# Fused mixer, expert lookup and delta-rule block: the 128x128 block inverses taken in two pairs of token blocks with the scan beside them, and the attention's division moved behind its value product

## Chip, cores and metric

The kernel runs on one core of a Trainium2 chip. The metric is the device time of one launch in microseconds. All data are f32; the big linear layers split every operand in two parts of fewer bits (`_hi` and `_lo`) and make three products of them, the smaller products named below are plain f32 products, which the profile counts as two matmul records each (a transpose is one record).

## What is computed

A first block (gated convolutions, a linear recurrence, a product-key expert lookup over 16384 experts) and then a second block, which alone is touched here. Its input is 512 tokens of width 1024; half of its width is causal attention with ALiBi slopes, the other half a gated delta rule:

```
moba_out = moba_attention(a_q, a_k, a_v) * silu(a_z)        # 8 heads of 64; 512 tokens: plain causal softmax
gdn_out  = rms_norm(gated_delta_rule(...), w) * silu(d_z)   # 4 heads of 128
mixed    = concat([moba_out, gdn_out]) @ w_out
return x + rms_norm(mixed, norm_post_w)

# gated delta rule, per chunk:
a     = strict_lower((k*beta) k^T * decay);  t_inv = (I + a)^-1
u     = t_inv @ (v*beta);   w = t_inv @ (k*beta*exp(gc))
v_new = u - w @ S
o     = (q*exp(gc)) @ S + intra @ v_new
S     = S*exp(g_last) + (k*exp(g_last - gc))^T @ v_new      # chunk after chunk
```

The attention's softmax is exp(logit - max), a sum over keys, and a division by the sum.

## The kernel before

Every engine runs its own instruction list; semaphores tie them together. For the second block all five lists are written by walking over one table, `STEPS2` (built by `second_block_steps`), so the table sets the order on every engine at once; an engine that has no part in a step passes over it. The stage of interest starts when the 32 input projections (`unit` 0 to 31) are over and ends with the first output projection (`unit` 32).

The 512 tokens are four blocks of 128 (`tb` 0 to 3); the delta rule's four heads of one block are handled together. Its steps:

- `M(level, tb)` and `X(level, tb)`: the inverse of I + a by doubling, 7 levels (0 to 6). `M` is eight 64x64 products (at level 6 four); ScalarE copies the result from PSUM to `M1[:, tb % 2]`; `X` is sixteen 64x64 products (level 6: four) with that copy; VectorE subtracts the result from the inverse. GpSimd writes the masked operand of the next level to `AO[:, tb % 2]` (`mask`). So a block's level is a circle: `M` on TensorE, copy on ScalarE, `X` on TensorE, subtraction on VectorE. At each level all four blocks pass, in the order M0 M1 X0 M2 X1 M3 X2 X3.
- `tokens(tb)`: transposes of k and v; VectorE makes `KB` and `VB` (4 + 4 `tensor_scalar`, one for each head, L2402), and ScalarE the decayed k (4 activations, L1817).
- `solve` (products w and u, copied by ScalarE), `read` (w @ S, VectorE subtracts: L2558), `scan` (o, and the product `su` that VectorE adds to the state: L2570, 4 instructions), `gsquare` (ScalarE's squares with sums, 4 instructions for each block, L1844), `groot` (ScalarE's square root L1850, VectorE's reciprocal and 12 or 4 scalings L2583), `gturn` (16 transposes, L1440, and four VectorE products L2588).
- `values(q)`: transposes of the attention's v.

The attention is cut into 32 pieces n (m = n // 8 a pair of heads, query block qb = n // 2 % 4, e = n % 2 the head), spread over 36 slots, one for each call of `attend()`, placed between the steps above. Slot i holds, in this order: `pv` of pieces i-5 and i-4 (odd i: the value product of both heads, L1471), `turn` of piece i-3 (transposes of the probabilities to PSUM bank 7, L1459, copied by ScalarE, L1865), `both_logits` of i and i+1 (even i, L1452), `logits` i (VectorE adds the slopes and takes the extreme, L2605; ScalarE takes exp with the sum, L1854), `probs` i-1 (VectorE's reciprocal L2610; ScalarE multiplies the row with it, L1859). After every eighth piece, at slots 11, 19, 27 and 35, the result of a head pair is gated and split: VectorE `tmp` (L2618), ScalarE `act_hi` (L1535), VectorE `act_lo` (L1914, in `rest`). This is called the head-pair switch below. Since VectorE works in order, the `logits` of that slot come after `act_lo`, and the next `both_logits` waits for them (`nm_ready`).

Small results share four PSUM banks in turn (`JOBS`, `bank`): job n waits with `wait_free` until job n-4 has been read (`emptied`).

## Time and profile before

| | |
|---|---|
| median of 3 runs | 1854.47 us (1851.41 to 1855.57) |
| the profiled execution's own time | 1854.16 us |
| its span in the trace | 1852.4 us |
| TensorE busy | 1792.7 us (97%) |
| VectorE, ScalarE, GpSimd busy | 1500.4, 721.3, 1048.3 us |
| stage from the first attention product to unit 32 | 1676.15 to 1789.69 us |

The profile's busy times count each instruction from start to end; TensorE's ends are modelled, and its instructions overlap a little, so for the cost of a group in a row the distance to the next group's start is the better measure (a group given with 1.10 us is followed 1.03 us later). `[0.58 <-DVE small L2605]` behind a row means that the engine stood idle 0.58 us before it and that this instruction released it. The clock column is the granted TensorE clock; 1.00 is 2.4 GHz, 0.50 is 1.2 GHz.

### The profile page before, as it was taken

To read this page: it belongs to the slowest core of one execution; us is meant where nothing else is said; L and a number is where in the kernel's file an instruction comes from. 1 tells how busy PE (TensorE), PEld (TensorE's weight loads), DVE (VectorE), ACT (ScalarE), POOL (GpSimd) and SP (SyncE) were. 2 spreads that over 40 slices of the span, in tenths; PEclk is the share of its full clock that TensorE was granted. 3 is DMA by queue.
4 is the path that set the end of the run, shared out by engine and by line. 5 is a ranking of instruction groups with operands and counts; after the bars stand their busy time and mean duration, and the time that the engine had idled before them with its cause. 6 is when DMAs were issued, how large, how long until landed. Compare 5 with 4: busy or idle time off the path is not lost.

```text
span 1852.4 us, 28952 instructions
## 1 busy us (share of the span) xinstructions
PE 1792.7 (97%) x10379; PEld 1566.0 (85%) x10379; DVE 1500.4 (81%) x2496; ACT 721.3 (39%) x1166; POOL 1048.3 (57%) x653
## 2 busy tenths in 40 slices
PE   7999999999999999999999999999999999999986
PEld 5788879999999999999888888888888686787765
DVE  5786899879998888888489999999999796655544
ACT  3454233333333444344333333333333434325652
POOL 1442355788888555555567777676775463336013
PEclk9999999999999999999999999999999999999998
DMA  9551524899999699899899999999997232210011
GB/s 373 202 172 57 185 77 137 280 318 318 327 319 312 233 305 320 296 309 318 326 339 360 362 356 363 349 363 357 368 353 273 69 92 79 69 57 2 2 57 57
DMA packets 159933, 440.48 MB, mean 238 GB/s; under 512 B 13664, under 2 KB 62944, under 8 KB 156768
## 3 DMA queue, kind: packets, MB, share of 16 engines
q1 hardware_dynamic: 64416, 254.71, 39.7%
q0 software_dynamic: 36864, 134.23, 19.3%
q10 hardware_dynamic: 58560, 50.34, 8.3%
q8 instruction: 54, 0.88, 0.2%
q14 instruction: 39, 0.32, 0.0%
HBM read 386.80 MB, written 52.43 MB: 237 GB/s over the span
## 4 chain that ended last, share of the span: by engine, by line
PE 88%; DVE 6%; DMA 2%; ACT 2%; issue 1%; SPq 0%; ACTq 0%; DVEq 0%
PE PS L974 15%; PE PS L983 15%; PE PS L975 15%; PE PS L1272 9%; PE PS L1273 9%; PE PS L1281 9%; PE PS L1239 4%; PE PS L1317 2%; PE PS L1001 1%; DMA arena<-in_w_ada 1%; PE PS L1308 1%; DVE arena L1946 1%; PE PS L1459 1%; PE PS L1452 1%; DMA gates_d<-arena 1%
## 5 line engine op out<-in xcount | busy, mean ns | idle before, releaser
L862 POOL TENSOR_TENSOR w_lo<-raw,w_hi 128x1024 fp32r<-128x1024 f32 x299 | 720.0, 2409 | 693.2 <-ACT w_hi L1502 692.2
L1502 ACT ACTIVATE w_hi<-raw 128x1024 fp32r<-128x1024 f32 x332 | 352.1, 1060 | 923.3 <-PE PS L983 570.7
L974 PE MATMUL PS<-act_hi,w_hi 128*128 128x384 f32 (+1 forms) x1584 | 576.4, 364 | 2.2 <-DVE act_lo L1914 0.7
L975 PE MATMUL PS<-act_lo,w_hi 128*128 128x384 f32 (+1 forms) x1584 | 562.8, 355 | 0.0
L983 PE MATMUL PS<-act_hi,w_lo 128*128 128x384 f32 (+1 forms) x1584 | 337.2, 354 | 0.0
L974 PEld LDWEIGHTS PS<-act_hi,w_hi 128*128 128x128 f32 x1584 | 299.0, 189 | 34.9 <-DVE act_lo L2379 4.9
L975 PEld LDWEIGHTS PS<-act_lo,w_hi 128*128 128x128 f32 x1584 | 299.1, 189 | 23.3 <-issue 2.6
L1272 PE MATMUL PS<-w_hi,act_hi 128*128 128x512 f32 x768 | 300.4, 391 | 3.4 <-ACT arena L1658 3.4
L983 PEld LDWEIGHTS PS<-act_hi,w_lo 128*128 128x128 f32 x1584 | 284.5, 188 | 22.6 <-issue 0.5
L1273 PE MATMUL PS<-w_hi,act_lo 128*128 128x512 f32 x768 | 300.2, 391 | 0.0
L2326 DVE TENSOR_TENSOR act_lo<-arena,act_hi 128x384 fp32r<-128x384 f32 x128 | 249.1, 1946 | 29.6 <-ACT act_hi L1716 29.6
L1281 PE MATMUL PS<-w_lo,act_hi 128*128 128x512 f32 x768 | 195.2, 389 | 0.0
L2181 DVE CUSTOM_DVE_ANT_0 arena<-arena,PS 128x1024 f32<-128x1024 f32 x128 | 153.8, 1213 | 25.5 <-DMA arena<-in_expert_u_rows,arena 25.2
L1272 PEld LDWEIGHTS PS<-w_hi,act_hi 128*128 128x128 f32 x768 | 145.0, 189 | 33.8 <-ACT arena L1658 3.7
L1273 PEld LDWEIGHTS PS<-w_hi,act_lo 128*128 128x128 f32 x768 | 145.0, 189 | 30.1
L1281 PEld LDWEIGHTS PS<-w_lo,act_hi 128*128 128x128 f32 x768 | 144.6, 188 | 30.1
L2298 DVE SCALAR_TENSOR_TENSOR PS<-arena,PS 128x1024 f32<-128x1024 f32 x127 | 162.4, 1279 | 0.5
L910 POOL DMA_INDIRECT arena<-in_expert_v,arena x128 | 134.9, 1054 | 24.8 <-issue 19.4
L2285 DVE TENSOR_TENSOR arena<-PS,arena 128x1024 f32<-128x1024 f32 x96 | 117.2, 1221 | 36.3 <-PE PS L1239 32.9
L910 POOL DMA_INDIRECT arena<-in_expert_u_rows,arena x128 | 122.4, 956 | 32.1 <-issue 12.0
L1239 PE MATMUL PS<-arena 128*128 128x128 f32 x768 | 93.5, 275 | 0.6 <-ACT arena L1694 0.4
L1239 PEld LDWEIGHTS PS<-arena 128*128 128x128 f32 x768 | 92.2, 191 | 1.1 <-ACT arena L1694 0.8
(358 smaller groups left out, 1913.2 us busy)
## 6 DMA issues: line engine op xcount, KB each, us to landing
raw<-in_expert_u SPq DMA_DIRECT2D x128, 512.0 KB, 5.4
raw<-in_expert_v SPq DMA_DIRECT2D x128, 512.0 KB, 5.9
raw<-in_w_in SPq DMA_DIRECT2D x52, 512.0 KB, 3.7
arena<-in_w_ada SPq DMA_DIRECT2D x24, 1024.0 KB, 9.6
gel_d<-arena ACTq DMA_DIRECT2D x64, 384.0 KB
gates_d<-arena ACTq DMA_DIRECT2D x12, 2048.0 KB, 15.4
arena<-gates_d SPq DMA_DIRECT2D x32, 768.0 KB, 7.0
arena<-gel_d SPq DMA_DIRECT2D x32, 768.0 KB, 8.8
```

The source lines that it names most:

```text
L862: pool.tensor_tensor(w_lo[:, k % SPLIT, :], raw[:, k % RAW, :], w_hi[:, k % SPLIT, :].bitcast(F32), ALU.subtract).then_inc(lo_split, 1)
L910: pool.indirect_dma_start(out=rows[buffer(s)], out_offset=None, in_=table, in_offset=bass.IndirectOffsetOnAxis(ap=row_i[:, s % SLOTS:s % S ...
L974: pe.matmul(own, w, act_hi[:, c, 0:n_tok], start=(i == 0), stop=False)
L975: pe.matmul(own, w, act_lo[:, c, 0:n_tok], start=False, stop=False)
L983: mm = pe.matmul(own, w_lo[:, k % SPLIT, c * P:(c + 1) * P], act_hi[:, c, 0:n_tok], start=False, stop=(i == KC - 1))
L1239: mm = pe.matmul(PS[:, 2 + g % 3, t * P:(t + 1) * P], hot[:, n, 0, :], hot[:, n, 1, :], start=True, stop=True)
L1272: pe.matmul(to, coef(act_hi, k)[:, q, :], w, start=start, stop=False, skip_group_check=True)
L1273: pe.matmul(to, coef(act_lo, k)[:, q, :], w, start=False, stop=False, skip_group_check=True)
L1281: mm = pe.matmul(PS[:, 2 * q + half, :], coef(act_hi, k)[:, q, :], w_lo[:, k % SPLIT, 512 * half:512 * half + 512], start=False, stop=stop ...
L1502: act.activation(w_hi[:, k % SPLIT, :], raw[:, k % RAW, :], ACT.Copy).then_inc(hi_split, 1)
L2298: v.scalar_tensor_tensor(out=own_ps, in0=rows[buffer(s)], scalar=dots[:, k:k + 1], in1=own_ps, op0=ALU.mult, op1=ALU.add).then_inc(rows_us ...
L2326: v.tensor_tensor(coef(act_lo, b % 4), craw[:, b % 2, :].rearrange("p (q t) -> p q t", q=GT), coef(act_hi, b % 4).bitcast(F32), ALU.subtra ...
```

## The change

1. Inverse. After level 0, which is as before, blocks 0 and 1 go through levels 1 to 6 alone (`invert_two(0, ...)`), then blocks 2 and 3. `tokens` 0 and 1 stand at the end of the first pair; `solve` 0 and 1, `read` 1, `scan` 0 and 1 and their `gsquare`, and `tokens` 2 and 3 stand inside the second pair's levels. Behind the inverse only blocks 2 and 3 are left of the scan.
2. Division. `probs` issues nothing any more. `turn` takes the undivided exp. One `precip` for each head pair takes 8 reciprocals at once; `prow` spreads them over 64 output rows for each head with 8 products against the identity (out 64x128), VectorE multiplies this into the gate `az`, and the switch multiplies the value product by that.
3. Tokens. `KB`, `VB` and the decayed k are three VectorE instructions of 128x512 with the scalars broadcast; ScalarE's four are gone. The k bank is free after the third.
4. Squares. `gsquare` of blocks 0 to 2 is one VectorE product and one reduction; block 3 stays on ScalarE.
5. The semaphore counts follow the table (`x_done`, `COPIED`, `MASKED`, `same_buffer_before`).

```
+        if i >= 10 and i % 8 == 2:
+            steps.append(("precip", i // 8 - 1))
         if i >= 4 and i % 2:
+            if i % 8 == 3 and i > 8:
+                steps.append(("prow", i // 8 - 1))
             steps.append(("pv", i - 4))
...
+    def invert_two(tb, between):
+
+        for level in range(1, LEVELS):
+            product(level, tb)
+            if level > 1:
+                steps.append(("X", level - 1, tb + 1))
+            steps.extend(between.get((level, 0), ()))
+            attend()
+            steps.append(("X", level, tb))
+            product(level, tb + 1)
+            steps.extend(between.get((level, 1), ()))
+            attend()
+        steps.append(("X", LEVELS - 1, tb + 1))
+
+    invert_two(0, {(5, 0): [("tokens", 0)], (6, 0): [("tokens", 1)]})
+    invert_two(2, {(1, 0): [("solve", 0)], (2, 0): [("read", 0), ("scan", 0), ("gsquare", 0)], (3, 0): [("solve", 1)],
+                   (3, 1): [("read", 1)], (4, 1): [("scan", 1), ("gsquare", 1)], (5, 0): [("tokens", 2)],
+                   (6, 0): [("tokens", 3)]})
+    for kind, n, count in (("solve", 2, 1), ("read", 2, 1), ("solve", 3, 0), ("scan", 2, 2), ("read", 3, 2), ("scan", 3, 2)):
         steps.append((kind, n))
         if kind == "scan":
             steps.append(("gsquare", n))
             if n == 3:
                 steps.append(("groot", 1))
-        if kind in ("tokens", "read", "scan"):
+        for _ in range(count):
             attend()
         if (kind, n) == ("read", 3):
             steps.append(("groot", 0))
...
-                    "kt": (tok_act, n + 1), "vt": (tok_dve, n + 1),
+                    "kt": (kd_ready, n + 1), "vt": (tok_dve, n + 1),
...
                 if kind == "turn":
-                    pe.wait_ge(p_ready, n + 1)
+                    pe.wait_ge(e_ready, n + 1)
...
+                if kind == "prow":
+                    pe.wait_ge(r_ready, n + 1)
+                    wait_free(pe, "pr", n)
+                    for q in range(TB):
+                        for e in range(2):
+                            k = 8 * n + 2 * q + e
+                            mm = pe.matmul(PS[64 * e:64 * e + 64, bank("pr", n), q * P:(q + 1) * P],
+                                           prec[:, k:k + 1].to_broadcast([P, 64]), ident[:, :], start=True, stop=True)
+                    full(mm, "pr", n)
...
-                if kind == "probs":
-                    w = (n // 2 % 4 + 1) * P
-                    act.wait_ge(r_ready, n + 1)
-                    act.activation(L[:, n % 3, 0:w], L[:, n % 3, 0:w], ACT.Copy, scale=prec[:, n:n + 1]).then_inc(p_ready, 1)
...
-                    per_head(KB[:, tb % 2, :], ("kt", tb), bge, 4 * tb)
-                    per_head(VB[:, tb % 2, :], ("vt", tb), beta, 4 * tb, last=tok_dve)
+                    own, kt = slice(4 * tb, 4 * tb + 4), h4(PS[:, bank("kt", tb), :])
+                    wait_full(dve, "kt", tb)
+                    v.tensor_tensor(h4(KB[:, tb % 2, :]), kt, by_head(bge[:, own]), ALU.mult)
+                    wait_full(dve, "vt", tb)
+                    v.tensor_tensor(h4(VB[:, tb % 2, :]), h4(PS[:, bank("vt", tb), :]), by_head(beta[:, own]),
+                                    ALU.mult).then_inc(tok_dve, 1)
+                    v.tensor_tensor(cv[:, 4:8, t], kt, by_head(egcum[:, 32 + 4 * tb:36 + 4 * tb]), ALU.mult).then_inc(kd_ready, 1)
...
+                if kind == "gsquare" and n < TB - 1:
+                    dve.wait_ge(o_ready, n + 1)
+                    chain.link(v.tensor_tensor(gscratch[:, :, :], otok[:, :, t], otok[:, :, t], ALU.mult))
+                    v.tensor_reduce(gsum[:, 4 * n:4 * n + 4], gscratch[:, :, :], AX_X, ALU.add).then_inc(gsq_ready, 1)
...
+                if kind == "prow":
+                    if n == 0:
+                        dve.wait_ge(z_done, 8)
+                    wait_full(dve, "pr", n)
+                    v.scalar_tensor_tensor(out=az[:, n, :], in0=PS[:, bank("pr", n), :], scalar=0.5, in1=az[:, n, :],
+                                           op0=ALU.mult, op1=ALU.mult).then_inc(gate_scaled, 1)
+                if kind == "precip":
+                    dve.wait_ge(e_ready, 8 * n + 8)
+                    v.reciprocal(prec[:, 8 * n:8 * n + 8], psum_[:, 8 * n:8 * n + 8]).then_inc(r_ready, 1)
```

**Order, TensorE at the third head-pair switch (slot 27).** In the kernel before, L1471 is `pv` of pieces 22 and 23, L1459 `turn` 24, L1426 and L1427 the eight products of `scan` 1, and L1308 its `su`; `turn` 25 and the next logits follow behind it.

```order
L1471 MATMUL PS<-arena,raw 64x128 [waits pt_ready]
L1471 MATMUL PS<-arena,raw 64x128 x7
L1459 MATMUL PS<-ident,arena 128x128 [waits pt_ready,p_ready]
L1426 MATMUL PS<-arena 128x128 [waits tok_dve,vn_ready]
L1427 MATMUL PS<-arena 128x128
```

In the changed kernel L1507 is `prow` 2, L1520 `pv`, L1499 `turn` 24 and 25, L1492 `both_logits` 28; the row ahead of L1507 is `su` of block 2.

```order
L1348 MATMUL PS<-arena 128x128 [waits vn_ready,kd_ready]
L1348 MATMUL PS<-arena 128x128 x3
L1507 MATMUL PS<-ident,small 64x128 [waits wu_ready,r_ready]
L1507 MATMUL PS<-ident,small 64x128 x7
L1520 MATMUL PS<-arena,raw 64x128 [waits pt_ready]
L1520 MATMUL PS<-arena,raw 64x128 x7
L1499 MATMUL PS<-ident,arena 128x128 [waits pt_ready,e_ready] x2
L1492 MATMUL PS<-arena 128x384 [waits nm_ready]
```

The scan's products stood behind the switch and stand ahead of it now; two turns and the next logits follow each other directly.

**Order, VectorE at the same place.** In the changed kernel L2609 adds `su` of block 2 to the state, L2615 and L2616 are the squares, L2655 is `prow`, L2666 `tmp`, L1945 `act_lo`, L2648 the logits of piece 27 (before, L2618, L1914 and L2605 stood with nothing of the scan ahead but L2558).

```order
L2609 SCALAR_TENSOR_TENSOR arena<-arena,small,PS 128x128 [waits bank_full2]
L2609 SCALAR_TENSOR_TENSOR arena<-arena,small,PS 128x128 x3
L2615 TENSOR_TENSOR arena<-arena 128x512 [waits o_ready]
L2616 TENSOR_REDUCE small<-arena 128x4 [waits dve_chain]
L2655 SCALAR_TENSOR_TENSOR arena<-PS,arena 128x512 [waits bank_full3]
L2666 TENSOR_TENSOR arena<-PS,arena 128x512 [waits pv_done,gate_scaled,alo_ready]
L1945 SCALAR_TENSOR_TENSOR act_lo<-arena,act_hi 128x512 [waits tmp_ready,ahi_ready]
L2648 ISA arena,small<-arena,PS 128x256 [waits pt_full,s_full]
```

The state, the squares and the spread sums now come ahead of the switch's `tmp` in this list.

**Order, ScalarE at the end of the stage.** Before: L1854 is the exp of piece 31, L1859 the last divisions, L1850 the square roots, L1844 the squares of block 3, L1865 the copies of `turn` 29 to 31.

```order
L1854 ACTIVATE arena,small<-arena,small 128x512 [waits nm_ready]
L1859 ACTIVATE arena<-arena,small 128x512 [waits r_ready]
L1850 ACT_TABLE_LOAD
L1850 ACTIVATE small<-small 128x12 [waits gsq_ready]
L1844 ACTIVATE arena,small<-PS 128x128 [waits bank_full2,gsq_ready]
L1844 ACTIVATE arena,small<-PS 128x128 [waits gsq_ready] x3
L1850 ACTIVATE small<-small 128x4 [waits gsq_ready]
L1865 ACTIVATE arena<-PS 128x384 [waits pv_done,pt_full]
```

Now: L1889 is exp (first row piece 30, last row piece 31), L1885 the square roots, L1879 the squares, L1896 the copies of `turn` 28 and 29.

```order
L1889 ACTIVATE arena,small<-arena,small 128x512 [waits nm_ready]
L1885 ACT_TABLE_LOAD
L1885 ACTIVATE small<-small 128x12 [waits gsq_ready]
L1879 ACTIVATE arena,small<-PS 128x128 [waits bank_full5,gsq_ready]
L1879 ACTIVATE arena,small<-PS 128x128 x3
L1885 ACTIVATE small<-small 128x4 [waits gsq_ready]
L1896 ACTIVATE arena<-PS 128x384 [waits pv_done,pt_full]
L1889 ACT_TABLE_LOAD
L1889 ACTIVATE arena,small<-arena,small 128x512 [waits nm_ready]
L1896 ACTIVATE arena<-PS 128x384 [waits pv_done,pt_full]
```

The square roots moved from behind the last exp to ahead of it; one more function table is loaded for that exp, and another for the square root at the kernel's very end (L1875 before, L1906 now).

## Rows read from the trace of the kernel before

**Rows 1.** Busy time by stretch: each engine's busy us, clock, DMA share, GB/s.

```profile
core 0 of [0], span 1852.4 us
...
1671.50:1676.15 4.65, 2.28 (x20) 1.69 (x17) 4.56 (x9) 2.72 (x5) 1.90 (x2) 1.00 0.00 0
1676.15:1742.44 66.29, 62.26 (x1220) 49.23 (x1219) 37.51 (x136) 42.01 (x121) 26.12 (x20) 0.97 0.01 3
1742.44:1770.43 27.99, 26.41 (x232) 23.09 (x231) 12.83 (x47) 21.54 (x68) 0.00 (x0) 1.00 0.01 2
1770.43:1789.69 19.26, 13.98 (x99) 10.47 (x97) 10.14 (x34) 9.93 (x31) 0.00 (x0) 0.82 0.00 0
1789.69:1852.40 62.71, 48.10 (x224) 39.08 (x222) 26.30 (x32) 18.34 (x28) 20.53 (x11) 0.91 0.25 84
```

**Rows 2.** The same view for two stretches at the lower clock.

```profile
1731.50:1735.30 3.80, 3.80 (x52) 2.91 (x48) 2.29 (x8) 2.30 (x8) 0.00 (x0) 0.55 0.00 0
...
1779.30:1786.10 6.80, 5.81 (x29) 4.56 (x30) 5.53 (x18) 1.13 (x3) 0.00 (x0) 0.51 0.00 0
```

**Rows 3.** Timeline of TensorE: start, us, instruction, idle time before it.

```profile
1700.79 1.61 PE L1317 MATMUL PS<-arena 64*64 64x64 f32 x48
1702.33 1.10 PE L1471 MATMUL PS<-arena,raw 128*64 128x128 f32 x16
...
1705.14 0.30 PE L1459 MATMUL PS<-ident,arena 128*128 128x128 f32 x1 [0.37 <-ACT arena L1865]
1706.02 0.92 PE L1452 MATMUL PS<-arena 64*128 64x384 f32 x4 [0.58 <-DVE small L2605]
...
1763.08 0.92 PE L1452 MATMUL PS<-arena 64*128 64x384 f32 x4
...
1767.17 0.44 PE L1459 MATMUL PS<-ident,arena 128*128 128x128 f32 x2
...
1770.75 1.13 PE L1452 MATMUL PS<-arena 64*128 64x512 f32 x4
1771.86 1.13 PE L1308 MATMUL PS<-arena 128*128 128x128 f32 x8
...
1778.71 0.30 PE L1440 MATMUL PS<-ident,arena 128*128 128x128 f32 x1 [2.54 <-DVE arena L2583]
```

**Rows 4.** Timeline of VectorE.

```profile
1703.47 0.69 DVE L2618 SCALAR_TENSOR_TENSOR arena<-PS,arena 128x512 f32<-128x512 f32 x1 [0.67 <-PE PS L1471]
1704.93 0.69 DVE L1914 SCALAR_TENSOR_TENSOR act_lo<-arena,act_hi 128x512 fp32r<-128x512 f32 x1 [0.77 <-ACT act_hi L1535]
1705.54 0.41 DVE L2605 CUSTOM_DVE_ANT_0 arena<-arena,PS 128x256 f32<-128x256 f32 x1
...
1725.81 2.15 DVE L2402 TENSOR_SCALAR raw<-PS,small 128x128 f32<-128x128 f32 x8
...
1763.08 1.12 DVE L2570 SCALAR_TENSOR_TENSOR arena<-arena,small,PS 128x128 f32<-128x128 f32 x4 [0.36 <-PE PS L1308]
...
1778.27 2.44 DVE L2583 TENSOR_SCALAR arena<-arena,small 128x128 f32<-128x128 f32 x12
...
1780.84 1.13 DVE L2583 TENSOR_SCALAR arena<-PS,small 128x128 f32<-128x128 f32 x4
```

**Rows 5.** Groups of VectorE over the span: the reduction of 512 columns.

```profile
L2269 DVE TENSOR_REDUCE arena<-arena 128x32 f32<-128x512 f32 x1 | 0.7, 686 | 3.1 <-ACT arena L1684 3.1
```

**Rows 6.** Timeline of ScalarE.

```profile
1704.20 0.63 ACT L1535 ACTIVATE act_hi<-arena 128x512 fp32r<-128x512 f32 x1 [0.92 <-DVE arena L2618]
...
1776.38 1.28 ACT L1850 ACT_TABLE_LOAD   x1
1777.67 0.30 ACT L1850 ACTIVATE small<-small 128x12 f32<-128x12 f32 x1
...
1836.85 0.26 ACT L1875 ACTIVATE arena<-PS,small 128x4 f32<-128x4 f32 x1 [1.14 <-PE PS L1014]
```

**Rows 7.** Groups of ScalarE from 1676.15 to 1789.69 us: the divisions.

```profile
L1859 ACT ACTIVATE arena<-arena,small 128x128 f32<-128x128 f32 (+3 forms) x32 | 17.7, 552 | 2.4 <-DVE small L2610 2.4
```

More of the change, by code:

```diff
@@ L114, in second_block_steps @@
     fill = 30
-    for level in range(LEVELS):
-        for what, tb in (("M", 0), ("M", 1), ("X", 0), ("M", 2), ("X", 1), ("M", 3), ("X", 2), ("X", 3)):
-            if (what, level) == ("X", 0):
-                steps.append((what, level, tb))
-            if what == "X":
-                if fill < 32:
-                    steps.append(("unit", fill))
-                elif fill == 33:
-                    steps += [("values", q) for q in range(TB)]
-                    attend()
-                elif fill > 33 and not (level == 6 and tb % 2):
-                    attend()
-                fill += 1
-            if (what, level) != ("X", 0):
-                steps.append((what, level, tb))
-            if (what, level, tb) in (("X", 5, 1), ("X", 6, 1)):
-                steps.append(("tokens", level - 5))
-            if what == "M" and 4 * level + tb + 2 < 4 * (LEVELS - 1):
-                steps.append(("mask", level + (tb + 2) // 4, (tb + 2) % 4))
@@ L136, in second_block_steps, with product @@
-    for kind, n in (("solve", 0), ("tokens", 2), ("solve", 1), ("read", 0), ("scan", 0), ("tokens", 3), ("solve", 2),
-                    ("read", 1), ("scan", 1), ("solve", 3), ("read", 2), ("scan", 2), ("read", 3), ("scan", 3)):
+    masks = iter([(0, 2), (0, 3)] + [(level, pair + tb) for pair in (0, 2) for level in range(1, LEVELS - 1) for tb in (0, 1)])
+    def product(level, tb):
+        steps.append(("M", level, tb))
+        if level < LEVELS - 1:
+            steps.extend(("mask", *at) for at in itertools.islice(masks, 1))
@@ new lines, in second_block_steps @@
+    for what, tb in (("M", 0), ("M", 1), ("X", 0), ("M", 2), ("X", 1), ("M", 3), ("X", 2), ("X", 3)):
+        if what == "M":
+            product(0, tb)
+        else:
+            steps.append(("X", 0, tb))
+            if tb < 2:
+                steps.append(("unit", 30 + tb))
+    steps += [("values", q) for q in range(TB)]
+    attend()
[9 more added lines that the diff above has]
+            steps.extend(between.get((level, 1), ()))
+            attend()
+        steps.append(("X", LEVELS - 1, tb + 1))
@@ L208, with x_done, same_buffer_before @@
 NAMES = list(JOBS)
+X_STEPS = [st[1:] for st in STEPS2 if st[0] == "X"]
+M_STEPS = [st[1:] for st in STEPS2 if st[0] == "M"]
+COPIED = [at for at in M_STEPS if at[0]]
+MASKED = [st[1:] for st in STEPS2 if st[0] == "mask"]
+def x_done(level, tb):
+    return TB + X_STEPS.index((level, tb)) + 1
+def same_buffer_before(order, level, tb):
+    own = [at for at in order if at[1] % 2 == tb % 2]
+    return own[own.index((level, tb)) - 1]
 class Chain:
@@ L949, in _ @@
                     if n or tb >= 2:
-                        before = (n, tb - 2) if tb >= 2 else (n - 1, tb + 2)
+                        before = same_buffer_before(MASKED, n, tb)
                         if before[0]:
@@ L953, in _ @@
                         else:
-                            pool.wait_ge(d_ready, TB + before[1] + 1)
+                            pool.wait_ge(d_ready, x_done(*before))
                     pool.tensor_tensor(h4(AO[:, tb % 2, :]), h4(AT[:, tb, :]),
@@ L1809, in _ @@
                     wait_full(act, "m", n, tb)
-                    act.wait_ge(d_ready, 4 * n + tb + 3)
+                    act.wait_ge(d_ready, x_done(*same_buffer_before(X_STEPS, n, tb)))
                     own = slice(0, P) if n < LEVELS - 1 else HI
                     act.activation(M1[own, tb % 2, 0:256], PS[own, bank("m", n, tb), 0:256], ACT.Copy).then_inc(m1_ready, 1)
-                if kind == "tokens":
-                    wait_full(act, "kt", tb)
-                    act.wait_ge(tok_dve, tb + 1)
-                    for h in range(GH):
-                        ins = act.activation(cv[:, 4 + h, t], PS[:, bank("kt", tb), h * P:(h + 1) * P], ACT.Copy,
-                                             scale=egcum[:, 32 + 4 * tb + h:33 + 4 * tb + h])
-                    ins.then_inc(tok_act, 1)
                 if kind == "solve":
@@ L1848, in _ @@
                     own = slice(0, 12) if n == 0 else slice(12, 16)
-                    act.wait_ge(gsq_ready, own.stop)
+                    act.wait_ge(gsq_ready, TB - 1 + 4 * n)
                     act.activation(grms[:, own], gsum[:, own], ACT.Sqrt, bias=eps, scale=1.0 / P).then_inc(g_root, 1)
```

61 lines of the change are left out of this document (28 added, 33 removed).

## Prediction

> **What bounds the kernel now.** I read the stretches first, then TensorE's timeline in them, then the lists of the engines it waits for. Outside the stage from 1676.15 to 1789.69 us the two programs issue the same steps, but for one table load at the end. The stage takes 113.54 us, and TensorE is busy in most of it: it is idle for 4.03, 1.58 and 5.28 us in its three stretches, 10.9 us together [rows 1]. In two places it also ran at the lower of its two levels, 1.2 GHz: a clock of 0.55 over 3.80 us costs 1.7 us, and 0.51 over 6.80 us, part of which was waiting anyway, about 2.5 us [rows 2]. That leaves 113.5 - 10.9 - 4.2 = 98.4 us of products at full clock, so the stage is bound by TensorE's own work, with 15.1 us to be had from waits and clock. The waits are short ones at the head-pair switch (0.37 and 0.58 us), where TensorE needs a copy and logits that stand behind `tmp`, `act_hi` and `act_lo`, and one of 2.54 us ahead of `gturn`, for VectorE's scalings behind the square root [rows 3]. The lower clock follows both kinds: a run of short waits before 1731.5 and the long one before 1779.3.
>
> **What the change adds.** `prow` is the only new work on the bound engine: 4 times 8 products of 128x128 onto 64 output rows. The nearest row is `pv` with 16 records, the same output, 1702.33 to its end 1.03 us on [rows 3]. A floor is half of it, a ceiling twice it (2 to 8 us); I take 4 x 1.03 = **4.1 us**, since size and record count are the same.
>
> **What it takes away, and who notices.** 32 divisions leave ScalarE (17.7 us [rows 7]) and the turns wait for one step less. But ScalarE is busy for 42.01 of 66.29 us in the first stretch and TensorE for 62.26 [rows 1]: the relief lies beside products and gives nothing by itself. The tokens stay as they are for VectorE (8 scalings 2.15 us; now three of 128x512, each 0.6 to the next start like 1704.93 to 1705.54 [rows 4], so 1.8 us and one more bank release at their end). GpSimd's masks are the same 22, in another order.
>
> **Two blocks in flight.** A block's circle is M 0.5 (a third of the 1.54 us that 48 records take), a copy, X 1.0, subtractions: about 3.0 us with hand-overs, an estimate. TensorE's period for one level of two blocks is 2 x 1.54 [rows 3] plus two attention slots of about 1 us: 5.1. So the circle has 2.1 us of slack, and the levels should stay filled. Exposed places, in program order:
>
> A. Level 1: X0 came behind M0 and M1 and comes behind M0 alone; the copy it needs is late by what M1 covered: +0.5.
>
> B. First switch, slots 11 and 12, right behind `tokens` 1. Counted from the end of X(5,1), VectorE has subtractions 1.2, tokens to 3.1, the gate times `prow` to 3.7, then `tmp` to the logits 2.07 us (1703.47 to 1705.54 [rows 4]) and 0.48 to the next `both_logits` (1705.54 [rows 4] to 1706.02 [rows 3]): 6.3. TensorE has in it about 4.7 us of work (transposes 1.0, `prow` and `pv` 2.06, two small turns 0.5, two steps of level 6 at an estimated 0.6). Wait 1.6.
>
> C. Last levels of the second pair. Between `su` 1 and M(5,3) VectorE must do state 1.1, squares 1.4, logits 0.3, subtractions 0.8, tokens 1.9: 5.5 us, because the k bank is now released by the third token instruction; TensorE has 4.9 there. Wait 0.6. At `tokens` 3 the same list delays logits 23, its exp and the copy of M(6,3): 0.9. Together 1.5.
>
> D. Behind `su` of block 2. The order shows that `prow`, `pv`, two turns and the next logits follow without cover, where `scan` 1 stood between before; and VectorE has state, squares and `prow` ahead of `tmp`. From the end of that `su`: state 1.1 [rows 4], squares 0.69 + 0.69 ([rows 5] for the reduction), less overlap 1.35, gate 0.6, switch 2.07, 0.48: **5.6 us**, against 2.6 us of TensorE's work. Wait 3.0. Then everything hangs in a line: logits 28 0.85, the read of block 3 0.95, value product and turn 0.4 each, 0.5 for a copy, turn 0.4, logits 30 1.06 [rows 3]: 10.1. Logits and exp of piece 30 1.6: 11.7. Table load and root up to the first scaling 1.89 (1776.38 [rows 6] to 1778.27 [rows 4]), the scalings 3.6 to the end of the last four: 17.2. Only now come logits 31 and its exp (1.55) and the copy of turn 29 (0.5), which stands behind that exp on ScalarE: 19.3. `pv` 29 0.8, turn 30 0.6, copy 0.7, turn 31 0.6, `prow` 3 over the copy 1.03, `pv` 31 1.03: **24.1 us** to unit 32. Before, the last `su` ended at 1770.43 and unit 32 began 19.26 us later [rows 1].
>
> **The table load.** Exp, root, exp makes two more loads than exp, root: one for exp 31, one for the root at the kernel's end. A load is 1.28 us, and the root begins 0.01 us after it [rows 6]. The first falls in the time in which ScalarE waits for logits 31. The second must fit in the 1.14 us that the last root waits [rows 6]: +0.15. The Trainium skill (ScalarE: Activation LUTs, What ACT_TABLE_LOAD costs) puts a drain of about 1.38 us beside each load, 2.66 us for a switch; this trace shows no such gap at this load. By the page the end would cost 1.5 instead of 0.15.
>
> **The sum.** Work outside the last stretch is 98.4 less that stretch's 11.5 (19.26 - 5.28 - 2.5), 86.9. Of it 3.2 us (`pv` 23 and 25, three turns, logits 28) move into D; two `prow` come in, 2.06; waits A, B, C 3.6. That is 89.4, with D 113.5 at full clock, where before it was 113.54. So without the clock the stage breaks even: what the waits of before give back, `prow` takes. For the clock I take two falls of 1.85, 3.7 us, since D has waits of 3.0, 2.2 (turn 29 behind the squares and root) and 1.9 us (`pv` 29), and one of 2.54 brought the clock down. Bounds: none, and 6 us. Total +3.7 + 0.15 = +3.8 on the profiled execution's own 1854.16 (the median is 1854.47, 0.3 above): **1858.0 us**, +0.2%.
>
> **Rivals.**
>
> Break-even: the same waits, but clock falls that lie in time that waits anyway, as in `gturn`, and slots that fill B. Then -2.5 to +1. For it: the 0.95 us of waits at the first switch cost no clock, since the whole first stretch ran at 0.97 [rows 1], which the 3.80 us of [rows 2] nearly account for.
>
> Faster: the switch and the square root are hidden. If of my waits only A, C and one of 2.3 us remain and the clock stays up, the stage is 98.4 + 4.1 + 4.3 = 106.8: -6.7, from -4 to -8. For it: ScalarE loses 17.7 us and half the scan is inside the levels. Against: the scan's cover is what it takes away from the tail, and squares of block 2 stand before the switch. It decides if VectorE's list at D is not late by more than 0.6 us.
>
> Starved levels: with two blocks instead of four, ScalarE's exp and turn copies stand between a product and its copy. Each 0.1 us over the 2.1 of slack in 24 half levels is 2.4 us; 0.25 gives +6 more, +9.8. Against: the in-order lists leave the copy ahead of the exp of the same slot.
>
> The drain: ScalarE would wait at each load, D longer by up to 1.4 and the end by 1.4: +5.2 to +6.6. The page named above gives this rule; the row's 0.01 us speaks against it.
>
> No effect of the regrouping, only `prow`: +4, inside the forecast's case.
>
> **How the numbers follow.** Forecast +1 to +7: 0.48. Break-even 0.24. Faster 0.14. Starved 0.09. Drain 0.05. About 0.2%, 3.7 us, is what a measurement can tell from no change. Faster by more: 0.14. Slower by more: half of the forecast's case 0.24, starved 0.09, drain 0.05: 0.38. The same: 0.48. The range runs from 1852.0, which leaves out the faster case, to 1863.0, which leaves out most of the starved one; the forecast's own is 1855 to 1861.
>
> **What the trace of the changed kernel would show.** `prow` at about 1.0 us each; hardly any idle TensorE between 1680 and 1695; a wait of 1 to 2 us at the first switch; after `su` of block 2 some 3 us of waiting released by ScalarE's copy and VectorE's logits; turn 29 and `pv` 29 waiting for ScalarE about 2 us each; a granted clock of 0.5 in one or two stretches behind these; a table load ahead of exp 31 that nobody waits for, and one ahead of the last root. The forecast is wrong if VectorE reaches the third switch's `tmp` on time, if the clock stays up, or if TensorE is idle in the levels themselves.

## The result and the profile after

The changed kernel takes 1859.78 us (median of 10 runs, 1856.68 to 1863.12), the kernel before in the same comparison 1854.63 (10 runs, 1850.73 to 1857.12): a ratio of 1.003, 95% interval 1.0021 to 1.0039. It is 5.2 us slower; the forecast was 3.8 us slower, inside its range, on the side that had 0.38 of the chance. The profiled execution took 1859.47 us, its span 1857.7.

First the stretches of the changed kernel (columns as in [rows 1]). The first three rows are the stage, cut at the end of the inverse and at the end of `su` of block 2; the fourth is what comes behind it, the fifth the whole stage. The last three are the stretches at the lower clock, cut by hand and a little short at their ends.

```profile
1676.15:1759.06 82.91, 78.23 (x1366) 63.69 (x1365) 45.89 (x128) 37.38 (x104) 26.54 (x20) 0.96 0.01 2
1759.06:1769.05 9.99, 9.99 (x90) 9.11 (x88) 1.94 (x7) 5.39 (x13) 0.00 (x0) 1.00 0.01 2
1769.05:1794.85 25.80, 19.12 (x158) 14.39 (x156) 15.16 (x44) 11.40 (x31) 0.00 (x0) 0.87 0.00 1
1794.85:1857.70 62.85, 48.12 (x224) 39.08 (x222) 26.30 (x32) 19.61 (x29) 20.54 (x11) 0.92 0.24 84
1676.15:1794.85 118.70, 107.34 (x1609) 87.20 (x1608) 62.99 (x179) 54.18 (x147) 26.54 (x20) 0.94 0.01 2
1676.90:1683.50 6.60, 5.97 (x93) 5.01 (x89) 1.68 (x8) 2.42 (x9) 3.17 (x4) 0.50 0.01 2
1775.90:1779.10 3.20, 3.17 (x14) 2.21 (x14) 1.21 (x3) 0.71 (x2) 0.00 (x0) 0.50 0.00 0
1786.20:1789.30 3.10, 3.10 (x14) 2.83 (x15) 3.06 (x13) 1.52 (x2) 0.00 (x0) 0.50 0.02 5
```

The stage starts where it did and lasts 118.70 instead of 113.54 us: 5.16 of the 5.3 us by which the span grew. TensorE is idle for 4.68 us in the levels and 6.68 in the last stretch, 11.4 against 10.9 [rows 1]. The middle stretch, where the block scan stands beside the last attention pieces, has no idle time at all. The granted clock is 0.94 of full over the stage, with three stretches at half clock; before it was 0.95, with the two of [rows 2].

TensorE's timeline, from level 1, from the first switch (slots 11 and 12), from the end of the levels, and from the third switch to unit 32 (a row's number before the engine is its us, the bracket the idle time ahead of it and who ended it):

```profile
1678.14 2.08 PE L1357 MATMUL PS<-arena 64*64 64x64 f32 x34 [0.63 <-ACT arena L1861]
...
1707.23 1.09 PE L1507 MATMUL PS<-ident,small 128*64 128x128 f32 x16 [0.53 <-DVE arena L2579]
...
1711.31 0.30 PE L1499 MATMUL PS<-ident,arena 128*128 128x128 f32 x1 [0.96 <-ACT arena L1896]
1712.06 0.92 PE L1492 MATMUL PS<-arena 64*128 64x384 f32 x4 [0.44 <-DVE small L2648]
...
1747.64 0.63 PE L1375 MATMUL PS<-ident,arena 128*128 128x128 f32 x4 [1.02 <-ACT arena L1861]
...
1758.45 0.68 PE L1357 MATMUL PS<-arena 64*64 64x64 f32 x8 [0.76 <-ACT arena L1861]
...
1769.13 1.09 PE L1507 MATMUL PS<-ident,small 128*64 128x128 f32 x16
1770.05 1.04 PE L1520 MATMUL PS<-arena,raw 128*64 128x128 f32 x16
1771.03 0.33 PE L1499 MATMUL PS<-ident,arena 128*128 128x128 f32 x1
1774.03 0.30 PE L1499 MATMUL PS<-ident,arena 128*128 128x128 f32 x1 [2.68 <-ACT arena L1896]
1774.92 0.92 PE L1492 MATMUL PS<-arena 64*128 64x384 f32 x4 [0.58 <-DVE small L2648]
...
1779.63 0.41 PE L1499 MATMUL PS<-ident,arena 128*128 128x128 f32 x2 [0.56 <-ACT arena L1896]
...
1786.18 0.87 PE L1499 MATMUL PS<-ident,arena 128*128 128x128 f32 x3 [2.03 <-ACT arena L1896]
1786.84 3.27 PE L1480 MATMUL PS<-ident,arena 128*128 128x128 f32 x16
1790.16 0.88 PE L1520 MATMUL PS<-arena,raw 128*64 128x128 f32 x12
```

Each of the four groups of `prow` is followed 0.90 to 0.93 us later: 3.7 us. The largest wait is the one behind the third switch, 2.68 + 0.58 us; VectorE and ScalarE say why:

```profile
1769.24 1.12 DVE L2609 SCALAR_TENSOR_TENSOR arena<-arena,small,PS 128x128 f32<-128x128 f32 x4 [4.24 <-PE PS L1348]
1770.28 0.68 DVE L2615 TENSOR_TENSOR arena<-arena 128x512 f32<-128x512 f32 x1
1770.99 0.69 DVE L2616 TENSOR_REDUCE small<-arena 128x4 f32<-128x512 f32 x1
1771.60 0.68 DVE L2655 SCALAR_TENSOR_TENSOR arena<-PS,arena 128x512 f32<-128x512 f32 x1
1772.37 0.69 DVE L2666 TENSOR_TENSOR arena<-PS,arena 128x512 f32<-128x512 f32 x1
1773.83 0.69 DVE L1945 SCALAR_TENSOR_TENSOR act_lo<-arena,act_hi 128x512 fp32r<-128x512 f32 x1 [0.77 <-ACT act_hi L1584]
1774.44 0.41 DVE L2648 CUSTOM_DVE_ANT_0 arena<-arena,PS 128x256 f32<-128x256 f32 x1
```

```profile
1746.52 0.62 ACT L1889 ACTIVATE arena<-arena,small 128x384 f32<-128x384 f32 x1 [2.56 <-DVE small L2648]
...
1747.13 0.36 ACT L1861 ACTIVATE arena<-PS 128x256 f32<-128x256 f32 x1
...
1773.09 0.63 ACT L1584 ACTIVATE act_hi<-arena 128x512 fp32r<-128x512 f32 x1 [4.15 <-DVE arena L2666]
1773.63 0.26 ACT L1896 ACTIVATE arena<-PS 128x128 f32<-128x128 f32 x1
...
1782.70 1.28 ACT L1885 ACT_TABLE_LOAD   x1
1783.99 0.30 ACT L1885 ACTIVATE small<-small 128x12 f32<-128x12 f32 x1
...
1786.05 1.28 ACT L1889 ACT_TABLE_LOAD   x1
1788.91 0.72 ACT L1889 ACTIVATE arena<-arena,small 128x512 f32<-128x512 f32 x1 [1.58 <-DVE small L2648]
...
1841.00 1.28 ACT L1906 ACT_TABLE_LOAD   x1
1842.30 0.26 ACT L1906 ACTIVATE arena<-PS,small 128x4 f32<-128x4 f32 x1
```

State, squares, spread sums and `tmp` run one behind the other without a gap. ScalarE stands still for 4.15 us ahead of `act_hi`, and the copy of turn 24 (L1896 at 1773.63), for which TensorE's turn 25 waits, is queued behind it. So TensorE waits for a copy of 0.26 us, but what is late is VectorE's list.

### The profile page after: what moved, and what is told of

Same layout as the page of the kernel before. It is cut to its first block and busy times, and to the rows that moved or that the text cites. A ratio compares the mean times of both kernels' runs of the same rounds, so it can differ in the third digit from the quotient of the medians.

```text
span 1857.7 us, 28970 instructions
## 1 busy us (share of the span) xinstructions
PE 1798.1 (97%) x10443; PEld 1570.1 (85%) x10443; DVE 1505.1 (81%) x2458; ACT 703.4 (38%) x1096; POOL 1050.2 (57%) x653
```

## The experiments

Twelve kernels, each timed beside the kernel before; an interval is the 95% interval of the ratio to it. The theory at the start was that of the prediction: TensorE pays for `prow`, the relief of ScalarE gives nothing by itself, and the regrouping costs waits in the last stretch and the clock that falls behind them.

**The division put back in the changed kernel.** `precip` and `prow` are taken out, `probs` issues again.

```
-        if i >= 10 and i % 8 == 2:
-            steps.append(("precip", i // 8 - 1))
-            if i % 8 == 3 and i > 8:
-                steps.append(("prow", i // 8 - 1))
-                    pe.wait_ge(e_ready, n + 1)
+                    pe.wait_ge(p_ready, n + 1)
+                if kind == "probs":
+                    act.wait_ge(r_ready, n + 1)
+                    act.activation(L[:, n % 3, 0:w], L[:, n % 3, 0:w], ACT.Copy, scale=prec[:, n:n + 1]).then_inc(p_ready, 1)
```

> The changed kernel with the division alone put back: ScalarE multiplies each row of probabilities with its reciprocal again, `precip` and `prow` are gone, the switch takes the gate as before. Theory (the spread sums cost what TensorE spends on them, the relief of ScalarE gives nothing): the 64 products of L1507, 3.7 us, go; in the last stretch the exp, reciprocal and division in a row give 0.5 to 1 us of it back. 1855.8 to 1857.5 us, against 1859.8. Rival (the pairs need the relieved ScalarE, copies of M come late behind exp and division): TensorE waits in the levels between 1684 and 1746 us, 1860 or more.

Measured: 1864.6 us (6 runs), ratio to before 1.0057 (1.0039 to 1.0075). Taking 3.7 us of products away made the kernel 4.8 us slower; this interval and that of the changed kernel (1.0021 to 1.0039) just meet. The theory falls for this kernel. The size is the rival's, the place only in part: in the levels up to the first switch no wait is added. The stage of this run, and its waits at the first switch, at the tokens of blocks 2 and 3, and at turn 29 and `pv` 29:

```profile
1671.78:1795.05 123.27, 107.38 (x1546) 86.25 (x1545) 62.35 (x203) 67.58 (x179) 26.42 (x20) 0.92 0.01 2
```

```profile
1706.12 0.30 PE L1496 MATMUL PS<-ident,arena 128*128 128x128 f32 x1 [1.53 <-ACT arena L1897]
...
1745.29 0.63 PE L1372 MATMUL PS<-ident,arena 128*128 128x128 f32 x4 [1.42 <-ACT arena L1858]
1752.25 0.63 PE L1372 MATMUL PS<-ident,arena 128*128 128x128 f32 x4 [0.68 <-ACT arena L1858]
...
1785.87 0.52 PE L1496 MATMUL PS<-ident,arena 128*128 128x128 f32 x3 [2.53 <-ACT arena L1897]
...
1790.47 0.88 PE L1517 MATMUL PS<-arena,raw 128*64 128x128 f32 x12 [1.57 <-ACT arena L1897]
```

Idle are 123.27 - 107.38 = 15.9 us instead of 11.4, and the clock is 0.92. At the tokens, at turn 29 and at `pv` 29 the copy that TensorE waits for now has a division ahead of it as well. At the first switch it stands behind `act_hi`, as in the changed kernel, and the waits there are the same in sum: 1.53 + 0.44 us, where the changed kernel has 0.53 + 0.96 + 0.44. Of the 4.5 us more of waiting, 3.4 lie behind the third switch. The stage is read from one execution, the fastest of the six (1859.53 us): it reached the stage 4.4 us earlier than that of the changed kernel, in a part where the two programs are alike, so the stages say +4.6 while these two executions took equally long.

**The division alone behind the value product.** The kernel before with `precip`, `prow`, the new `turn` and the new switch.

```
+        if i >= 10 and i % 8 == 2:
+            steps.append(("precip", i // 8 - 1))
+            if i % 8 == 3 and i > 8:
+                steps.append(("prow", i // 8 - 1))
-                    act.activation(L[:, n % 3, 0:w], L[:, n % 3, 0:w], ACT.Copy, scale=prec[:, n:n + 1]).then_inc(p_ready, 1)
```

> The kernel before with the division alone moved behind the value product; inverse, scan, tokens and squares as before. Theory: four groups of L1507's products at 0.93 us add 3.7 us, less at most 0.5 for turns that wait for one step less: 1857.8 to 1858.3 us, against 1854.6. Rival (the turns' shorter chain closes waits of TensorE, the 5.3 us idle of the last stretch among them): 1854.6 or less. Together with the run that undoes the division this says what the pairs alone cost: by the theory 1.5 to 2 us on either side.

Measured: 1855.15 us (12 runs) against 1854.53, ratio 1.0002 (0.9991 to 1.0014).

```profile
1676.72:1790.06 113.34, 104.58 (x1610) 85.19 (x1609) 61.20 (x193) 60.06 (x186) 26.10 (x20) 0.97 0.01 2
```

The stage is as long as before, with 64 more records for `prow`: idle time went from 10.9 to 8.8 us and the clock from 0.95 to 0.97. In this execution the products are paid by closed waits, which is the rival's mechanism, and in as large a part by the clock; the time is not told from no change.

**Squares of block 2 behind the switch.**

```
-        if kind == "scan":
-            steps.append(("gsquare", n))
-            if n == 3:
-                steps.append(("groot", 1))
+        if kind == "scan" and n == 3:
+            steps += [("gsquare", 3), ("groot", 1)]
         for _ in range(count):
             attend()
+        if (kind, n) == ("scan", 2):
+            steps.append(("gsquare", 2))
```

> The changed kernel with the squares of block 2 (L2615 and L2616, 1.37 us on VectorE) behind the logits of piece 28 instead of ahead of the third switch. Theory (VectorE's list is what is late there): the wait of 3.26 us behind `su` of block 2 becomes 1.9 us, and since everything behind it hangs in a line the time falls by 1.2 to 1.4 us, to 1858.5 us. Rival (another chain is as late, or the clock falls anyway and eats it): 1859.5 to 1860.

Measured: 1857.58 us (12 runs), ratio 1.0022 (1.0009 to 1.0034). The wait ahead of `turn` 25 is 1.55 instead of 2.68 us, with 0.58 behind it as before, so VectorE's list is what is late there. The median fell by 2.2 us, but its interval overlaps that of the changed kernel, and this run's profiled stage (118.66 us) has 3.4 and 10.2 us at half clock: the mechanism is shown in the trace, its price in time is not settled.

**The waits filled.** Products that nobody reads, in PSUM bank 6, ahead of `turn` 24 and 29.

```
+        FILLED = {24: 10, 29: 7}
...
+                    if n in FILLED:
+                        pe.wait_ge(nm_ready, n // 2 * 2 + 3 if n < 28 else 31)
+                        for _ in range(FILLED[n]):
+                            pe.matmul(PS[:, 6, 0:P], ones[:, :], ones[:, :], start=True, stop=True)
```

> The changed kernel with 10 products of ones with ones (128x128, result read by nobody) ahead of `turn` 24 and 7 ahead of `turn` 29, in time in which TensorE waits. Theory (the two falls of the clock in the last stretch come from these waits and cost about 1.3 us each beyond the waits): granted clock 1.00 from 1769 to 1790 us, 1857 to 1858 us. Rival 1 (the low clock lies in time that waits anyway): 1.00 too, but 1859.5. Rival 2 (the fall comes of chance with no regard to these waits): the clock still falls. In every run of this set that begins the stage as the changed kernel does, the start of level 1 (1676.8 to 1683.5 us in the changed kernel's trace) shows whether the low clock there is the change's or one execution's.

Measured: 1858.56 us (12 runs), ratio 1.0022 (1.0011 to 1.0033). The long wait lay ahead of `turn` 25; the ten products stand one step earlier, and 0.46 and 0.53 us of the two waits there are left. The whole stage, the start of level 1, and the end of the stage:

```profile
1676.50:1793.84 117.34, 108.30 (x1644) 88.61 (x1643) 63.02 (x179) 54.23 (x147) 26.51 (x20) 0.97 0.01 2
1676.90:1683.60 6.70, 6.01 (x92) 5.03 (x92) 1.69 (x8) 2.46 (x10) 3.28 (x3) 0.53 0.01 2
1774.00:1790.00 16.00, 12.48 (x99) 9.23 (x98) 10.16 (x34) 9.75 (x29) 0.00 (x0) 1.00 0.00 1
```

The clock stays at 1.00 where it fell twice, and the stage is 1.4 us shorter in this execution; the medians differ by 1.2 us, which their intervals don't separate. The fall at the start of level 1 is still there. One execution could be chance, but the other profiles bear it out for the first of the two waits: of the eight kernels in pairs, the four that neither fill nor cover the wait behind the third switch (the changed kernel, `rows_divided`, `squares_behind`, `root_late`) all have low clock from 1774 to 1776 us on, and the four that do (`waits_filled`, `all_filled`, `scan_covers`, `pairs_covered`) have none there. The wait at turn 29 is followed by a fall in some executions (`scan_covers`, `pairs_covered`) and by none in `rows_divided`, where it is 2.53 us. Together the two falls cost about 1.4 us, not 3.7.

**The order of before under the changed code.** `second_block_steps` is that of the kernel before, with `precip` and `prow`; all else is the changed kernel's.

```
-    invert_two(0, {(5, 0): [("tokens", 0)], (6, 0): [("tokens", 1)]})
...
+    for level in range(LEVELS):
+        for what, tb in (("M", 0), ("M", 1), ("X", 0), ("M", 2), ("X", 1), ("M", 3), ("X", 2), ("X", 3)):
...
```

> The changed kernel's code (division behind the value product, tokens and squares on VectorE) over the order of steps of the kernel before, so all but the regrouping. The runs so far say that the division moved alone costs nothing (1855.15 against 1854.53). Theory (the regrouping into pairs is what costs, by its cover taken from the last stretch): 1854 to 1855.5 us, no wait of over 2 us at the third switch. Rival (the tokens' third instruction and the squares on VectorE make its list late, in whatever order): 1857 us or more, with waits released by VectorE between 1745 and 1770 us that the run of the division alone doesn't have.

Measured: 1851.45 us (12 runs) against 1854.78, ratio 0.9985 (0.9974 to 0.9997): below the expected range, and 8.3 us below the changed kernel.

```profile
1677.46:1787.45 109.99, 103.06 (x1609) 84.01 (x1609) 63.26 (x179) 52.64 (x146) 26.09 (x20) 0.98 0.01 2
```

The same 1609 products as in the changed kernel in 109.99 instead of 118.70 us. Idle: 6.9 instead of 11.4. Clock: 0.98 instead of 0.94, 2.2 us lost instead of 7.1. The regrouping is the loss; between these two executions half of the difference is waits and half clock, and 3.0 us of the clock's part are the fall at level 1, which comes and goes from execution to execution (see below).

**Scan 2 as cover of the third switch.**

```
-    for kind, n, count in (("solve", 2, 1), ("read", 2, 1), ("solve", 3, 0), ("scan", 2, 2), ("read", 3, 2), ("scan", 3, 2)):
+    for kind, n, count in (("solve", 2, 1), ("read", 2, 1), ("solve", 3, 1), ("scan", 2, 1), ("read", 3, 2), ("scan", 3, 2)):
```

> The changed kernel with `scan` 2 and its squares behind slot 27, so that its products stand between the third switch and `turn` 25, as those of `scan` 1 did before. Theory (VectorE's list ahead of the switch's `tmp` makes the wait): the 2.68 and 0.58 us released by ScalarE's copy and VectorE's logits shrink to some 1 us together, 1857.5 to 1858.5 us against 1859.8. Rival (the state then comes as late as the switch did, and `read` 3 and the root wait instead): 1859.5 to 1860.5 us.

Measured: 1854.29 us (12 runs), ratio 1.0002 (0.999 to 1.0013): 5.5 us below the changed kernel, from one line of the order. The squares of block 2 move with the scan.

```profile
1674.57:1789.14 114.57, 105.53 (x1609) 85.88 (x1608) 62.85 (x179) 53.91 (x147) 26.49 (x20) 0.96 0.01 2
```

```profile
1770.79 1.13 PE L1348 MATMUL PS<-arena 128*128 128x128 f32 x8 [0.31 <-issue]
...
1773.63 0.41 PE L1499 MATMUL PS<-ident,arena 128*128 128x128 f32 x2 [0.98 <-ACT arena L1896]
...
1780.17 0.52 PE L1499 MATMUL PS<-ident,arena 128*128 128x128 f32 x3 [2.02 <-ACT arena L1896]
```

Of the 2.68, 0.58 and 0.56 us behind the switch 0.31 and 0.98 are left, and the clock doesn't fall there; the 2.02 us at turn 29 stay, with a fall of 3.4 us behind them. In the two profiled executions the stage is 4.1 us shorter. The theory's mechanism held, its size was too small, since it counted no clock.

**The root behind the exp of piece 31, as before the change.**

```
-    for kind, n, count in (("solve", 2, 1), ("read", 2, 1), ("solve", 3, 0), ("scan", 2, 2), ("read", 3, 2), ("scan", 3, 2)):
+    for kind, n, count in (("solve", 2, 1), ("read", 2, 1), ("solve", 3, 0), ("scan", 2, 2), ("read", 3, 3), ("scan", 3, 1)):
```

> The changed kernel with `groot` 0, `scan` 3 and `groot` 1 behind the exp of piece 31, as before the change; one function table load less before unit 32 and one less at the kernel's end. Theory (the root stands in a line either way; the wait of 2.03 us ahead of `turn` 29 goes and one of about 3 us ahead of `gturn` comes, as in the kernel before): within 0.7 us of 1859.8, less 0.17 at the end: 1859 to 1860. Rival (squares, root and table load between the exps of pieces 30 and 31 are what holds up the tail): 1857.5 or less.

Measured: 1862.07 us (6 runs), ratio 1.0043 (1.0028 to 1.0059): 2.3 us slower, outside both expectations. The 2.03 us ahead of turn 29 went, and 1.92, 0.39, 0.46 and 0.73 us ahead of `gturn` came. So the early root looks like a gain, also with the two table loads that it adds, but the intervals of the two kernels overlap and the profiled execution lost more to the clock than the changed kernel's (0.93 over the stage).

**The waits in `values` filled as well.**

```
+                    if tb >= 2:
+                        pe.wait_ge(rms_ready, 20)
+                        for _ in range(2 * tb - 1):
+                            pe.matmul(PS[:, 6, 0:P], ones[:, :], ones[:, :], start=True, stop=True)
```

> The run with the filled waits (1858.56 us) and, beyond it, 3 and 5 products of ones in the two waits of TensorE inside `values` (0.93 and 1.44 us, which the kernel before has too). Theory (the low clock at the start of level 1 comes from these waits, by chance of where an execution stands, not from the changed order): no low clock at the start, 1855.5 to 1857.5 us, since it costs about 3 us in the executions that have it. Rival (it comes from the wait of 0.69 us for the copy of M(1,0), which the change makes): still there, 1858.5.

Measured: 1858.98 us (12 runs), ratio 1.0018 (1.0003 to 1.0033), no less than without. In the profiled execution the clock holds at the start, and falls for 3.4 us at 1713.0, behind the first switch, instead.

**Tokens and squares alone moved to VectorE.** The four-block kernel above with the division put back, by the first experiment's edit.

> The order of the kernel before, its division too, and only tokens and squares moved to VectorE: the fourth corner beside before (1854.8), division alone (1855.2) and the four blocks in flight with all three (1851.5). Theory (the three moves to VectorE bring 3 us by themselves, since ScalarE's token activations and late copies were what TensorE waited for behind `tokens` 1): 1851 to 1852.5. Rival (only a ScalarE freed of both makes its copies on time): 1854 to 1855.5.

Measured: 1849.26 us (11 runs) against 1854.33, ratio 0.9976 (0.9967 to 0.9986): 5.1 us faster than before, more than the theory had. The profiled execution was the slowest of the eleven (1853.62 us), with the low clock from 1778 us to the end of the stage; its stage is 110.61 us all the same.

```profile
1678.53:1789.14 110.61, 101.98 (x1546) 82.47 (x1545) 62.87 (x203) 65.72 (x178) 26.07 (x20) 0.95 0.01 2
```

Between 1742 and 1758 us it has no wait, where the kernel before had 0.74 and 0.80 us for copies of ScalarE:

```profile
1748.96 0.52 PE L1459 MATMUL PS<-ident,arena 128*128 128x128 f32 x3 [0.74 <-ACT arena L1865]
...
1754.94 0.63 PE L1459 MATMUL PS<-ident,arena 128*128 128x128 f32 x4 [0.80 <-ACT arena L1865]
```

Its idle time is 8.6 us against 10.9: 2.3 of the 5.1 us are waits that closed. The rest this trace does not show, as it is that of the slowest execution, and tokens and squares were not moved one without the other.

**Four blocks and the early root.**

```
-        if kind in ("tokens", "read", "scan"):
+        if kind in ("tokens", "read", "scan") and (kind, n) != ("read", 3):
             attend()
+        if (kind, n) == ("scan", 3):
+            attend()
         if (kind, n) == ("read", 3):
             steps.append(("groot", 0))
```

> The four blocks in flight (1851.45) with root, `scan` 3 and squares of block 3 ahead of slot 31 instead of behind it, as the changed kernel has them. By the run with the late root, which was 2.3 us slower than the changed kernel, the early root is worth 2 us: 1849 to 1850.5, the waits of 1.38, 0.39, 0.46 and 0.73 us ahead of `gturn` gone, one of 2 us ahead of `turn` 29 in their place. Rival (the gain was the clock's by chance): 1851 to 1852.5.

Measured: 1849.53 us (11 runs), ratio 0.9981 (0.997 to 0.9991), 1.9 us below the same kernel with the late root, which the two intervals don't separate.

**Both repairs of the pairs.** Scan 2 behind slot 27 and its squares behind slot 28, by the edits above.

> The changed kernel with `scan` 2 behind slot 27 (which gave 1854.3) and its squares behind slot 28 (which alone gave 1857.6, that is 2.2 us less). Theory (once the switch is covered VectorE is on time, so the squares cost nothing more): 1853.5 to 1854.5. Rival (the two add up): 1852 to 1852.8.

Measured: 1855.12 us (12 runs), ratio 1.0013 (1.0004 to 1.0021). The wait ahead of turn 27 is 0.57 instead of 0.98 us and the time is not less: they don't add up. The medians alone would make it 0.8 us slower than the cover alone, which their intervals don't separate.

**Tokens and squares on VectorE, and the early root.**

> Order and division of the kernel before, tokens and squares on VectorE (1849.3), and root, `scan` 3 and squares of block 3 ahead of slot 31. In the four-block kernel with the moved division that early root was worth 1.9 us (1851.45 to 1849.53). Theory (the parts add): 1847 to 1848 us, faster than both kernels by more than 0.3%; the waits ahead of `gturn` (2.30, 0.39, 0.46 and 0.73 us) shrink to about 1 us together. Rival (the division in the turns' chain, which the early root makes longer by an exp, takes it back): 1849 to 1850 us.

Measured: 1848.08 us (6 runs) against 1856.24, ratio 0.9962 (0.9949 to 0.9974). This is the lowest median, faster than both kernels; the parts added nearly as expected. The early root came out ahead in all three pairs of kernels (2.3, 1.9 and 1.2 us), each time with intervals that overlap.

```profile
1674.56:1782.23 107.67, 98.94 (x1545) 80.75 (x1544) 62.75 (x203) 67.06 (x179) 26.08 (x20) 0.98 0.01 2
```

## Why the prediction was right, and where it was not

The parts of the change, from the medians. Each number is the kernel's own median; before it was 1854.3 to 1854.8 beside most of them.

| order | division | tokens, squares | us |
|---|---|---|---|
| four blocks | rows | ScalarE (before) | 1854.6 |
| four blocks | behind | ScalarE | 1855.2 |
| four blocks | rows | VectorE | 1849.3 |
| four blocks | behind | VectorE | 1851.5 |
| pairs | rows | VectorE | 1864.6 |
| pairs | behind | VectorE (changed) | 1859.8 |
| pairs, scan 2 behind slot 27 | behind | VectorE | 1854.3 |

So the change is three: tokens and squares -5.3, the division then +2.2, the pairs +8.3; together +5.2. The first and the last are clear of noise, the +2.2 is not: the intervals of its two kernels (0.9967 to 0.9986 and 0.9974 to 0.9997) overlap. The work itself is nearly the same: stage less idle time less what the clock took (one minus the clock, times the stage) is 97.0 us before, 97.5 in the pairs with rows divided, and 101.2, 100.9 and 100.2 in the three runs with `prow` (division alone, four blocks, changed). All the rest is waits and clock. (The clock is given to 0.01, so each of these is good to 0.6 us.)

By the prediction's steps:

- **What bounds the stage**: right. 98.4 us of products were named; 97.0 come out by the rounded clock, which charges the low clock also for the time that waited anyway.
- **`prow` 4.1 us**: 3.7. The same row of `pv`, taken at 1.03 us for each, was a little dear.
- **"The relief lies beside products and gives nothing by itself"**: this step failed. "The tokens stay as they are for VectorE" is right for that engine, but ScalarE's four activations for each block, which leave its list, were given no worth, nor were the squares. Moving tokens and squares off ScalarE brought 5 us alone. The division cost 0.6 alone instead of its 3.7 us of products, and in the pairs its relief was worth 3.7 + 4.8 = 8.5 us. ScalarE was busy for 42.01 of 66.29 us [rows 1], but a busy share does not say whether one short copy is late: many of TensorE's waits are for copies of 0.3 to 0.5 us that stand behind something else.
- **Why the sum came out all the same**: it added up the waits that remain, place by place, and in that the relief is contained. Idle time was put at 3.6 us in A to C and 7.1 in the last stretch with the switch at 3.0 (3.0 + 2.2 + 1.9), and measured at 4.68 and 6.68. Part of the nearness is luck. The 1.9 us of `pv` 29 did not come, and 0.56 and 0.78 us ahead of turns 27 and 31, which were not named, stand in their place. The clock was to cost 3.7 us where 4.2 had been lost, so 0.5 less than before; by the rounded clock it cost 1.4 more than before, and `prow` with the rest of the work 3.2 instead of 4.1. And the sum gives no part its own price: that a gain of 5 us and a loss of 8 lay in it is nowhere in the prediction.
- **A, +0.5**: 0.63. **B, 1.6**: 0.53 + 0.96 + 0.44 = 1.93. **C, 1.5**: 1.02 + 0.17 + 0.76 = 1.95, but not all as argued. The first wait is not for the k bank's third reader; it is ScalarE's copy of M(5,2) (L1861 at 1747.13), behind the exp of slot 20 (1746.52), whose logits ScalarE had awaited for 2.56 us.
- **D, a wait of 3.0**: 3.26, with the named parts one behind the other. Taking the squares away shortened it by 1.13, and putting `scan` 2 into it removed most of the wait and the clock's fall, 5.5 us by the medians. That is the main loss, and the order's rows showed it ahead of time. Turn 29: 2.03 for 2.2. `pv` 29 did not wait for its copy: `gturn` ran at half clock for 3.27 us over the same time. Unit 32 came at 25.8 us, the two falls included, for 24.1 without them.
- **The clock, 3.7 us in two falls**: two falls came in D, as named, but holding the clock there gave 1.4 us in the stage. The profile has one more stretch, from 1676.9 to 1683.5, that was not named: 6.60 us at 0.50 with 5.97 of work, 3.0 us. With the 0.63 us of A before it I first took it for the change's. It begins at 1676.9, ahead of that wait, where TensorE had issued the same products at the same times as before. Seven of the fourteen profiled executions have a fall at that place, among them the two four-block kernels with the early root; seven have none. So a fall at that place is no mark of the pairs. How often the clock falls in the levels is another matter. Ahead of the third switch all eight kernels in pairs have low clock, 3.4 to 7.0 us of it (17 with the division on ScalarE), six of them from 1706 to 1713 us on, at the first switch; of the six in four blocks three have none, three have 3.5 us, and none has it at the first switch. There the pairs wait 1.93 us, the kernel before 0.95. This is one execution of each kernel, and no run fills the first switch alone.
- **Table loads**: right. Each is 1.28 us, followed by its activation 0.01 to 0.02 us later, or by a wait for logits (1.58 us) that begins when it is over. From the last square to the last root 0.17 us more than before, for 0.15. The Trainium skill (ScalarE: Activation LUTs, What ACT_TABLE_LOAD costs) puts a drain of about 1.38 us beside each load; by that, an estimate, the end would have grown by 1.5, and this trace doesn't have it.
- **The rivals**: starved levels did not come (no wait between 1684 and 1704 us), break-even and faster neither. What was missed is that a mixture of them lay in the change: a gain of 5 us that never showed, because the pairs took more.

What stays open: why the clock at the start holds in one execution and falls in another, and why holding it there gave no time; how the 8.3 us of the pairs split beyond the 5.5 that the cover of the switch gave back, though the clock in the levels and the longer wait at the first switch are the candidates; and which of tokens and squares brought the gain.

## What to carry to other kernels

A change of several parts is to be priced part by part against each other, not only as a sum: here -5, +2 and +8 made +5, and the gain alone, with an earlier root, was the best kernel at 1848.1 us. Where an in-order engine is busy half of the time, ask for each wait of the bound engine what stands ahead of the one short instruction that it waits for: taking work off that queue can be worth more than its price on the bound engine (here 8.5 us for 3.7, in the pairs). And when a schedule moves products forward, look at what they used to cover: the switch lost its cover, and one line that put it back gave 5.5 us.

## What the runs showed of the hardware

The stretches of TensorE at a granted clock of 0.50 lasted about 3.4, 6.9, 10.3 or, in `moved_to_vector`, 13.7 us, with or without waits inside them. In the changed kernel a wait of 2.68 us and one of 2.03 were each followed by one, and products that nobody reads, 10 and 7 of them in these waits, held the clock at 1.00 without lengthening the kernel. Where it falls is not fixed by the program: products that start at equal times from 1669.66 to 1676.57 us, in the kernel before and the changed one, ran on at 1.00 in one execution and fell to 0.50 in the other. The 6.6 us at level 1 hold back 3.0 us of work, and ten runs of the kernel before spread over 6.4 us.
